# Block ends of a two-network forward pass: the last four output products reordered by token half and columns, norm scale and offset applied behind the transposes, the residual moved to GpSimd in the next block

## The reference, cut to what matters

```
# first network, last step:
h = rmsnorm(x, norm_pre_ffn) * (1 + sc_f) + sh_f
y = conv_ffn(h, f_up_w, f_dw_w, f_dw_b, f_down_w)     # width 2816
x = x + gt_f * rmsnorm(y, norm_post_ffn)
# second network, i = 0, 1:
x = layer_norm(ALPHA*x + 0.5*swiglu(x, ffn1...[i]), ln_g[i,0], ln_b[i,0])
proj = x @ w_in;  mix = rwkv7_mix(...) if i == 0 else stick_breaking_mix(...)
heads = concatenate([mix, memory_attention(...)])
x = layer_norm(ALPHA*x + heads @ w_out[i], ln_g[i,1], ln_b[i,1])
x = layer_norm(ALPHA*x + 0.5*swiglu(x, ffn2...[i]), ln_g[i,2], ln_b[i,2])
# swiglu(x, g, u, d) = (silu(x @ g) * (x @ u)) @ d
# layer_norm(x, g, b) = (x - mean) * rsqrt(var + 1e-5) * g + b
```

## Time and profile before

| | |
|---|---|
| three runs | 1635.96, 1639.16, 1644.09 us |
| the profiled execution's own time, its span | 1636.73 us, 1635.0 us |
| mean granted TensorE clock | 0.936 of full speed |
| TensorE busy | 1456.0 us, 89% of the span |
| VectorE, ScalarE, GpSimd busy | 936.2, 657.0, 195.1 us |
| DMA | 257.48 MB, mean 157 GB/s |

### The profile page before, as it was taken

How to read it: one execution, slowest core, us unless ns; L and a number is a source line. 1 busy time by engine, 2 the same in 40 slices (tenths; PEclk the granted TensorE clock), 3 DMA queues, 4 the chain that set the end, 5 groups by cost and what they waited for, 6 DMA issues and landing times. The chain is left out here.

```text
span 1635.0 us, 30811 instructions
## 1 busy us (share of the span) xinstructions
PE 1456.0 (89%) x12484; PEld 1326.4 (81%) x12484; DVE 936.2 (57%) x1140; ACT 657.0 (40%) x795; POOL 195.1 (12%) x189
## 2 busy tenths in 40 slices
PE   6999799997999968939867999979999795799996
PEld 4777699997999968828857999979999794599995
DVE  3565576666555554675546555565555538455555
ACT  4545545454333335532323333433333335243331
POOL 1440223322000030012311000010000002100000
PEclk8999899998999979969978999989999897799998
DMA  9955466665666534300035666646665340476661
GB/s 362 357 175 196 132 195 186 182 192 142 192 184 180 162 117 148 103 0 4 4 103 159 188 189 181 182 143 189 182 192 167 103 155 1 132 217 190 183 191 38
DMA packets 297511, 257.48 MB, mean 157 GB/s; under 512 B 6880, under 2 KB 274144, under 8 KB 294368
## 3 DMA queue, kind: packets, MB, share of 16 engines
q1 hardware_dynamic: 297440, 256.44, 52.4%
HBM read 255.37 MB, written 1.05 MB: 157 GB/s over the span
## 5 line engine op out<-in xcount | busy, mean ns | idle before, releaser
L137 PE MATMUL ps<-actT,a_parts 128*128 128x256 f32 x2176 | 625.5, 287 | 19.7 <-DVE actT L338 11.0
L138 PE MATMUL ps<-actT,a_parts 128*128 128x256 f32 x2176 | 622.1, 286 | 0.0
L139 PE MATMUL ps<-actT,a_parts 128*128 128x256 f32 x2176 | 621.7, 286 | 0.0
L137 PEld LDWEIGHTS ps<-actT,a_parts 128*128 128x128 f32 x2176 | 424.3, 195 | 31.4 <-issue 20.4
L138 PEld LDWEIGHTS ps<-actT,a_parts 128*128 128x128 f32 x2176 | 424.3, 195 | 3.9
L139 PEld LDWEIGHTS ps<-actT,a_parts 128*128 128x128 f32 x2176 | 423.9, 195 | 0.0
L967 DVE TENSOR_TENSOR a_parts<-a_raw,a_parts 128x2048 fp32r<-128x2048 f32 x100 | 240.4, 2404 | 76.1 <-ACT a_parts L964 75.9
L978 DVE TENSOR_TENSOR b_parts<-b_raw,b_parts 128x1024 fp32r<-128x1024 f32 x80 | 98.0, 1225 | 174.0 <-ACT b_parts L975 174.0
L964 ACT ACTIVATE a_parts<-a_raw 128x2048 fp32r<-128x2048 f32 x100 | 190.0, 1900 | 0.3 <-DMA a_raw<-in_ffn_w_up 0.3
L122 DVE TENSOR_TENSOR a_parts<-a_raw,a_parts 128x2048 fp32r<-128x2048 f32 x53 | 126.6, 2388 | 105.2 <-ACT a_parts L118 105.2
L975 ACT ACTIVATE b_parts<-b_raw 128x1024 fp32r<-128x1024 f32 x100 | 105.7, 1057 | 185.8 <-PE ps L139 185.8
(11 more groups left out here) (309 smaller groups left out, 1552.1 us busy)
## 6 DMA issues: line engine op xcount, KB each, us to landing
a_raw<-in_ffn_w_gate SPq DMA_DIRECT2D x88, 512.0 KB, 4.0
a_raw<-in_ffn_w_up SPq DMA_DIRECT2D x88, 512.0 KB, 5.2
b_raw<-in_ffn_w_down SPq DMA_DIRECT2D x88, 512.0 KB, 3.6
arena<-in_mod_w SPq DMA_DIRECT2D x24, 1024.0 KB, 8.9
a_raw<-in_f_up_w SPq DMA_DIRECT2D x44, 512.0 KB, 5.4
b_raw<-in_f_down_w SPq DMA_DIRECT2D x22, 512.0 KB, 3.6
a_raw<-in_rwkv_w_in SPq DMA_DIRECT2D x10, 1024.0 KB, 5.5
a_raw<-in_sb_w_in SPq DMA_DIRECT2D x10, 1024.0 KB, 5.1
```

The costliest lines, as they stand in the source:

```text
L137: pe.matmul(out, lhs[0], rhs[0], start=start, stop=False)
L138: pe.matmul(out, lhs[0], rhs[1], start=False, stop=False)
L139: return pe.matmul(out, lhs[1], rhs[0], start=False, stop=stop)
```

## The change

It has these parts.

1. In `ffn_stage` the loop ends one turn earlier. On TensorE both last up tiles come first, then the 48 products of the last four tiles (`down_block`), ordered so that the sums of (token half 0, columns 0), (0, 1), (1, 0) are each finished and announced (`acc_done`) before (1, 1). The eight transposes of token half 0 stand in the queue inside block (1, 1), before its last two tiles. The last turn's down weights are split into slot 1 of `a_parts`, the last two hidden tiles into two new slots of `hid`.
2. The norm's scale and offset by g and b are applied after the transposes, as per-partition columns of `par`; `x_tok` then holds the norm without them. Half of the columns are made by VectorE (`block_low`), half by ScalarE (`block_high`). The second token half is turned, scaled and split at the start of the next block (`turn_tokens(pe, got, 1)`, `take_tokens`); the first product there takes input columns 4 to 7 first (`K_TURNED`).
3. GpSimd makes the residual xs from that `x_tok` with the earlier norm's rows: per token half a multiplication by g, an addition of b, a multiplication by ALPHA. It waits for the rows' DMAs.
4. In the last stage SyncE waits for xs, then loads the rows of the last norm, and only then comes to the loop of weight loads. The output is stored in four pieces within the block.
5. `output_stage` runs chunks 2 and 3 by output block; chunk 2 is split into `b_parts`.

The core of the diff (the conv branch and the parts that follow the same pattern are cut):

```diff
+        HALF = [slice(0, 512), slice(512, D)]
+        K_TURNED = [4, 5, 6, 7, 0, 1, 2, 3]
+        BLOCKS = [(0, 0), (0, 1), (1, 0), (1, 1)]
+        def block_sum(dve, i, t, n, yb, xs, scale, end):
+            wait_block(dve, i, t, n, end)
+            dve_steps.step(dve, dve.scalar_tensor_tensor(yb[:, t, HALF[n]], acc[t][:, HALF[n]], scale,
+                                                         xs[:, t, HALF[n]], ALU.mult, ALU.add))
+            dve_steps.mark(dve.bn_stats(stats[:, t, 6 * n:6 * n + 6], yb[:, t, HALF[n]]))
+        def block_low(dve, i, t, yb):
+            block_scale(dve, i, t)                       # waits for the root, reciprocal
+            dve.scalar_tensor_tensor(stats[:, t, 15:16], stats[:, t, 12:13], -1.0, stats[:, t, 14:15], ALU.mult,
+                                     ALU.mult).then_inc(shift_out[t], 1)
+            dve.tensor_scalar(x_tok[:, t, HALF[0]], yb[:, t, HALF[0]], stats[:, t, 12:13], stats[:, t, 14:15],
+                              ALU.subtract, ALU.mult).then_inc(low_ready[t], 1)
+        def block_high(act, i, t, yb):
+            act.wait_ge(shift_out[t], i)
+            act.activation(x_tok[:, t, HALF[1]], yb[:, t, HALF[1]], ACT.Identity, bias=stats[:, t, 15:16],
+                           scale=stats[:, t, 14:15]).then_inc(high_ready[t], 1)
+        def turn_tokens(pe, i, t):
+            for h, ready in enumerate((low_ready[t], high_ready[t])):
+                pe.wait_ge(ready, i + 1)
+                for k in range(4 * h, 4 * h + 4):
+                    ins = pe.transpose(turned_at(i, t, k), x_tok[:, t, k * P:(k + 1) * P], ident[:])
+                ins.then_inc(token_turned[t], 1)
+        def norm_act_side(act, i, yb, norm):
+            block_root(act, i, 0)
+            block_high(act, i, 0, yb)
+            first_affine(act, ..., range(6), ...)        # six 128x128 activations
+            block_root(act, i, 1)
+            block_high(act, i, 1, yb)
+        def norm_dve_side(dve, i, yb, xs, scale, norm, end):
+            dve.wait_ge(pool_out.sem, pool_out.at("xs"))
+            block_sum(0, 0); block_sum(0, 1); block_stat(0); block_low(0)          # arguments cut
+            block_sum(1, 0); block_sum(1, 1); block_stat(1)
+            first_affine(dve, ..., range(6, KD), ...)    # two 128x128 tensor_scalars
+            block_low(dve, i, 1, yb)
+        def take_tokens(i, yb, norm):
+            def on_act(act):
+                tokens_act(act, i, 1, yb, norm)          # four affine activations, one copy of 128x512
+            def on_dve(dve):
+                ...
+                    dve.tensor_copy(actT[:, 0, :, first], token_view(yb, 0)).then_inc(token_hi[0], 1)
+                    dve.tensor_tensor(actT[:, 1, 0:4, first], ..., ALU.subtract).then_inc(token_lo[0], 1)
+                tokens_affine(dve, i, 1, yb, norm)       # four 128x128 tensor_scalars behind the transposes
+                tokens_hi(dve, 1, yb, norm)              # one copy of 128x512
+                tokens_lo(dve, i, 1, yb, norm)           # two subtractions of 128x512
+            def on_pool(pool):
+                if norm is not None:
+                    pool.wait_ge(token_hi[0], i + 1)
+                    pool.tensor_tensor(actT[:, 1, 4:KD, first], ..., ALU.subtract).then_inc(token_lo[0], 1)
+        def residual(pool, xs, norm, rows_at):
+            if norm is None:
+                pool.tensor_scalar(xs, x_tok[:], ALPHA, None, ALU.mult).then_inc(pool_out.up("xs"), 1)
+                return
+            pool.wait_ge(rows_loaded, rows_at)
+            for t in range(NT):
+                pool_steps.step(pool, pool.tensor_tensor(xs[:, t], x_tok[:, t], rows[:, 0], ALU.mult))
+                pool_steps.step(pool, pool.tensor_tensor(xs[:, t], xs[:, t], rows[:, 1], ALU.add))
+                ins = pool.tensor_scalar(xs[:, t], xs[:, t], ALPHA, None, ALU.mult)
+            ins.then_inc(pool_out.up("xs"), 1)
 # ffn_stage, SyncE, in front of the loop of weight loads
+                    if last:
+                        sp.wait_ge(pool_out.sem, pool_out.at("xs"))
+                        load_row(sp, 0, norm_row("g", norm))
+                        load_row(sp, 1, norm_row("b", norm))
                     with sp.Fori(1, BODY) as j:
 # ffn_stage, TensorE
-                    down_pe(pe, 1, BODY - 1, False, True)
-                    if turn_x:
-                        turn_x_pe(pe)
+                    up_pe(pe, 0, BODY - 2)
+                    down_pe(pe, 1, BODY - 3, False, False)
+                    up_pe(pe, 1, BODY - 2)
+                    up_pe(pe, 0, BODY - 1)
+                    up_pe(pe, 1, BODY - 1)
+                    tiles = [(q, j) for j in (BODY - 2, BODY - 1) for q in range(2)]
+                    early = [((t, n), tile) for t, n in BLOCKS[:3] for tile in tiles[:2]]
+                    late = [((t, n), tile) for t, n in BLOCKS[:3] for tile in tiles[2:]]
+                    for (t, n), tile in early + late + [(BLOCKS[3], tile) for tile in tiles]:
+                        ...
+                        if (t, n) == BLOCKS[3] and tile == tiles[2] and not last:
+                            turn_tokens(pe, hand, 0)
+                        ins = down_block(pe, *tile, t, n, False, tile == tiles[-1])
 # ffn_stage, conv only: GpSimd splits tile (0, BODY - 1), VectorE (1, BODY - 1) behind it
+                    if conv:
+                        dve.wait_ge(ring_b.lo_done, sb_ + NF - 1)
+                    split_b(None, dve, 1, BODY - 1)
 # output_stage
+                        if c > 2:
+                            act.wait_ge(ring_a.used, g0 + (2 if c == 3 else 1))
+                        act.activation(parts_of(c, 0), a_raw[:, (g0 + c) % 2], ACT.Copy).then_inc(ring_a.hi_done, 1)
+                    for t, n in BLOCKS:
+                        for c in range(2, 4):
+                            if t == 0 and n == 0:
+                                ring_a.wait_split(pe, g0 + c)
+                            if t == 1 and n == 1 and c == 3:
+                                turn_tokens(pe, hand, 0)
+                            ins = down_chunk(pe, parts_of, c, t, n)
```

More of the change, by code:

```diff
@@ L898, in build_program, with ffn_stage @@
         done = {"h": 0, "f_step": 0, "conv": 0, "gated": 0}
-        def ffn_stage(name, conv, norm_rows, turn_x, next_a, next_b, take):
+        def ffn_stage(name, conv, norm, hand, next_a, next_b, take):
             cg, cu, hf, yb, xs = carve((2, SEQ), (2, SEQ), (2, SEQ), (NT, D), (NT, D))
+            last = norm == 5
+            end = (ring_b.used, sec[name, "B"] + NF)
+            got, got_norm = take[2:4] if take is not None else (None, None)
             ga, gb = sec[name], sec[name, "B"]
@@ L953, in _ @@
                         ring_b.load(sp, g)
+                    if last:
+                        for t in range(NT):
+                            for n, ready in enumerate((low_ready[t], high_ready[t])):
+                                sp.wait_ge(ready, hand + 1)
+                                sp.dma_start(out[0, t * P:(t + 1) * P, HALF[n]], x_tok[:, t, HALF[n]])\
+                                    .then_inc(out_stored, 16)
                 def count(ring_first, q, j, back=0):
@@ L1073, in _ @@
                 def _(pe):
+                    if take is not None:
+                        turn_tokens(pe, got, 1)
                     up_pe(pe, 0, 0)
@@ L1203, in ffn_views @@
+            if not last:
+                return take_tokens(hand, yb, norm)
         def ffn_views(gate, up_w, down):
@@ L2033, in stick_stages @@
             g0 = sec["sb_in"]
-            act_at = [act_steps.n + c for c in range(10)]
-            expect_input()
+            act_at = [act_steps.n + 1 + c for c in range(10)]
+            got = take[2]
             expect_memory()
```

464 lines of the change are left out of this document (273 added, 191 removed).

## The result

The changed kernel takes 1657.05 us (median of 4 runs, 1649.81 to 1658.38), the kernel before 1640.68 in the same comparison (4 runs). The ratio is 1.0088, with a 95% interval of 1.0056 to 1.0120: slower by 16.4 us. The forecast was 1655 (1634 to 1670). The profiled execution took 1649.81 around a span of 1648.1, so it is 13.1 above that of before. It is also the fastest on record: the other three are 6 to 9 above it, and two further executions took 1651.55 and 1655.09.

A forecast was written before the change was run, and what follows sets the result against it. TensorE, computing for 89% of the span, was taken to lose time in pauses at block ends. Terms 11.4 + 4.9 - 2.9 - 7.6 - 4.0 - 18.0 = -16.2, from the median 1639.2: 1655 us, eight in ten between 1634 and 1670.

The forecast's parts named there:

- Part 6: Last stage: SyncE's wait for xs delays weight loads; TensorE 15.7 us idle plus 2.3 for lower clock, 18.0 lost.
- Part 2: Last end: VectorE ends 6.3 us behind the last product instead of 11.4; 4.9 saved, store as before.
- Part 1: Three layer-norm ends: sums and statistics overlap the last down products; 9.5 against 13.4 us, 3.8 saved each, 11.4 together.
- Rival 4: Block ends: the new order brings nothing because VectorE meets other work and ends when it did; 1666 us, chance 0.06.
- rival 2: Block ends: the clock does not fall; 1634 us, or 1619 with Rival 1; chance 0.14 alone or with Rival 1.
- Part 4: Two output stages: chunk 3's split leaves TensorE 3.0 us idle and xs comes late; 3.8 lost each, 7.6 together.
- Part 5: Starts of `ffn2` 0 and `ffn1` 1: GpSimd's residual passes hold up VectorE; 2.0 us lost each, 4.0 together.
- The sign that the prediction named: First turns: VectorE casts of 256 columns longer than 0.29 us.
- Part 3: Conv end: late weight splits leave TensorE 2.0 and 3.5 us idle, partly offset behind the end; 2.9 lost.
- Rival 1: Shared port: no meeting of GpSimd's passes with VectorE costs anything; 1639 us, no change, chance 0.20.
- Rival 3: Shared port: VectorE and GpSimd alternate strictly from a stage's start; 1670 us, chance 0.14.
- the subtraction of the earlier trace: VectorE's two-input subtraction beside GpSimd's scaling took 2.88 us instead of 2.29 and ended before the scaling's recorded end.

The follow-up runs named there:

- e1_rows_late: Changed kernel, but in the last stage SyncE's wait for xs and the last norm's row loads stand behind the loop of weight loads: 1638.47 us.
- e2_out_early_late: Changed kernel, but output stages run chunk 2's products for three blocks, then chunk 3's for them, then the last block: 1657.14 us.
- e3_out_one_scaling: Changed kernel, but in both output stages GpSimd makes xs with one scaling, leaving out the earlier norm's g and b: 1644.74 us.
- e5_no_alpha: Changed kernel without GpSimd's two ALPHA passes; the sums take 1/ALPHA and the root eps/ALPHA^2 instead, same result: 1644.43 us.
- e7_ffn_one_scaling: `e1_rows_late`, plus xs by one scaling without g, b or a wait for rows in `ffn2` 0, `ffn1` 1, `ffn2` 1: 1650.30 us.
- e6_all: Changed kernel with `e1_rows_late`, `e2_out_early_late`, `e5_no_alpha`, VectorE alone for last conv low parts, output stages' next-chunk split behind first half's norm: 1626.47 us.

## Why the prediction held, by its steps

**Part 6 (18.0 lost).** The mechanism is shown, by the timeline and by `e1_rows_late`. From the stage's first product to its last the profiles give 208.6 instead of 188.0, 20.6 lost: the pause was 17.17 instead of 15.7, and 3.4 (forecast 2.3) are restart and the rest. xs came at B + 24.5: six passes from B + 5.3 took 19.2 together, where I had 15.3 and 5 of meetings from B + 4.1. That both end at B + 24.5 is part luck: the rows came 1.2 later and the passes cost 1.1 less. From there the load took longer: ScalarE's copy started at B + 34.1, not B + 33.

**Part 2 (4.9 saved).** VectorE ended 6.9 behind the start of the last product (11.7 before), 4.8 saved; from the product's end that is 6.7, forecast 6.3. (The prediction's own 11.4 - 6.3 is 5.1, not the 4.9 that it sums.) I took the store behind it as unchanged; it was not. The span ends 2.4 behind VectorE instead of 4.7: the output is stored in pieces as they are made, and no block ends in between. That is 2.2 more. This unforeseen 2.2 makes up for most of part 6's 2.6 too many: 20.6 - 7.0 = 13.6 for the stage, where 13.1 was forecast. Here two misses cancel.

**Part 1 (3.8 each, 11.4).** 3.2, 4.6 and 3.9, together 11.7. The step sum of one end, 8.25 behind the products, was 8.4. Rival 4 (no overlap) is out by the same rows; rival 2 (clock stays up) too: from 596.60 to 601.30 the granted clock averaged 0.50. Its edge, a fall 3.6 behind the last product, was read from one end; here the fall came 2.4 behind it, so the shorter pieces didn't keep the clock up.

**Part 4 (3.8 each, 7.6).** 4.5 and 4.3. The forecast's 866 for xs and 881.8 for the next first product stand on the time axis of before, where the stage starts at 840.29; here it starts at 839.18. So xs came 27.1 behind the stage's first product and not 25.7, the next first product 42.2 and not 41.5: the near agreement of 866.29 and 881.41 with the forecast is luck. The pause before chunk 3 was 5.16, not 3.0: the split met a GpSimd pass, a meeting that I counted for xs but not for the split. `e2_out_early_late` shows that this pause is hidden behind xs, so the miss cost nothing. `e3_out_one_scaling` and `e5_no_alpha` show what xs costs.

**Part 5 (4.0 lost): the failed step.** It reads "I take 2.0 lost in each of `ffn2` 0 and `ffn1` 1". The meetings took place: at the start of the last stage two splits of `b_parts` took 6.77 where two took 2.35 before:

```profile
1434.96 2.35 DVE L122 TENSOR_TENSOR b_parts<-b_raw,b_parts 128x1024 fp32r<-128x1024 f32 x2
```

The sign that the prediction named is there too: the first cast of 256 columns took 0.61 in the changed kernel, 0.30 before. But TensorE did not stop for them: between the first product and the block's end no pause over 0.35 stands in either stage, in any of the eight profiled executions with all six passes. `ffn2` 0 and `ffn1` 1 gained as much as an end without the passes (4.6 and 3.9 against 3.2), and `e7_ffn_one_scaling` found the same body without the passes (`ffn1` 1: 197.76 against 197.8 to 198.4). The term is 0 to within some 0.5 a stage, not 2.0. `ffn2` 0 varies more, 197.7 to 199.6 with the same passes; the long executions have up to 6.1 us at the lower clock at its start, the short ones 2.8. The cover is thin, though: in `e5_no_alpha` and `e6_all`, where two passes are gone and the others follow closer, pauses of 0.4 to 1.5 appear and the stages are up to 2 longer.

**Part 3 (2.9 lost).** 2.0 in the first pair of profiles, 2.0 to 3.8 over the eight profiled executions with this end unchanged (204.4 to 206.2, against 202.4). Of the pauses, the first was 0.7 and not 2.0, twice (0.67, 0.70), the second 2.59 and not 3.5, and 0.62 for the transposes. What I left out is the clock behind the 2.59: in the first profile products ran at the lower level for about 3.4 us there, which by the clock's half costs about 1.7 (an estimate).

**Rivals 1 and 3.** Rival 1 (no meeting costs anything) is out: the splits of 4.43 and 6.77 are meetings, and xs lost 6 to them in `output_stage(0)` (21.1 for passes of 15.1). What the prediction counted for it, GpSimd's splits of 2.49 in the conv stage, misses who paid: VectorE's splits that fell beside them took 2.88 instead of 2.29. Rival 3 has the mechanism right for two-input passes, turns taken strictly, but prices it on TensorE's path, where only xs and chunk 3's split are. (Its own terms sum to 29, not to the 31 that it adds.)

**Not forecast: the rwkv mixer, 3.1 shorter.** Its second weight chunk is late at its start. Before, the product at 610.52 stood for 3.19 behind a split behind a load, which landed at 606.21:

```profile
610.52 0.58 PE L137 MATMUL ps<-actT,a_parts 128*128 128x256 f32 x1 [3.19 <-DVE a_parts L122]
```

In the changed kernel the same place shows 0.74, behind one of 0.51 (timeline):

```profile
598.41 12.59 SPq L112 DMA_DIRECT2D a_raw<-in_rwkv_w_in  x3
...
606.78 0.39 PE L137 MATMUL ps<-actT,a_parts 128*128 128x256 f32 x1 [0.51 <-DVE a_parts L122]
...
610.66 0.39 PE L137 MATMUL ps<-actT,a_parts 128*128 128x256 f32 x1 [0.74 <-DVE a_parts L122]
```

The barrier now falls 4.7 before the first product instead of 1.5, and the loads that a block issues at its start, here from 598.41 on, hide behind transposes and scaling. Work moved from one side of a barrier to the other makes the DMAs of the new block early. I counted the move as time on the path alone. The gain lies all at this start: from the mixer's first product to the end of a pause of 1.38 that both kernels have, it was 33.65 before and is 30.49 now, and 30.3 to 31.4 in all eleven profiled executions with the new ends. The 1.9 less of pause is one part; the lower clock that stood behind the 3.19 (0.57 from 610.0 to 614.0, 1.00 in the changed kernel from 611 to 615) is another. No experiment moves the barrier alone, so the cause is argued from the rows. Behind this start the mixer varies: it lasts 237.5 to 241.5 over these executions, so in some of them nothing of the gain is left.

**The sum.** 16.2 slower was forecast, 16.4 was measured. In the profiles it is 13.1, of which 3.3 lie up to the conv stage, in the first network's mixer, where no edit explains them; over all the variants that stretch lasts 194.3 to 198.0. Without them the stages show 9.8 where the terms said 16.2. So the sum is right partly by luck, by offsetting errors: part 5 (4.0 too much) and the rwkv mixer (3.1 unforeseen gain) lie on one side, the mixer's 3.3 and the median's distance from the profiled execution (7.2, against 2.5 to 4.0 before) on the other. Why the other executions of the changed kernel are 2 to 9 slower than the one profiled stays open; the stretches that vary most between profiled executions are the mixers (110.0 to 113.5, 237.5 to 241.5) and the unchanged output stages (42.1 to 43.8).

## What to carry to other kernels

A wait that is put into an in-order queue is paid by everything behind it: here one semaphore wait (with two row loads) in front of a loop of loads cost 19.8 us, more than the 11.7 that three well-shortened ends brought, and the same lines behind the loop cost nothing visible. Before a pass moves to GpSimd, look at which VectorE instructions it can meet and who is first; delete the pass if algebra allows, as with the scaling that a norm cancels. When a pause in the profile looks like the loss, take it away once: if the stage keeps its length, the limit is the next wait in the chain.

## What the hardware showed that I had not expected

- GpSimd and VectorE exclude each other for whole instructions in both directions, and 0.1 us of order decides who pays: split 2.29 or 4.43, pass 2.40 or 4.46. It is very regular. In the twelve traces 345 of VectorE's weight splits were issued while a GpSimd pass with two inputs ran, and each ended as if it had started 0.13 to 0.15 before that pass's end. The 160 passes of 1024 columns that were issued within such a split, 56 of them scalings with one input, ended as if they had started 0.11 to 0.18 before the split's end. The Trainium skill, SBUF — State Buffer, section Who interferes with whom, has this rule for two-input VectorE instructions, and the traces agree with it wherever GpSimd's pass had two inputs.
- A one-input scaling of GpSimd that came first held a cast of VectorE for all of its recorded 5.36 us (cast 4.97), though the subtraction of the earlier trace rows beside the same kind of scaling lost only 0.6. The prediction says that this subtraction ended before the scaling's recorded end; the rows have it the other way round, 1435.03 against 1434.63, so 0.40 behind. A block to the end would still have made it 2.3 behind. This too is regular: of 77 splits issued while such a scaling ran, the 24 that came more than 2.2 before its recorded end ended as if they had started 1.88 before it, and the 53 that came in its last 1.5 lost nothing. Why a cast is held longer than a subtraction stays open.
- At the conv end a pause of only 2.6 us was followed in each of the eight profiled executions by products at a lower granted clock (0.57 to 0.74 in the lower of two windows of 4 us); the pause of 1.91 in the one execution of before by none, one of 1.53 in one execution of three.
